# Sums of squares of keys and queries: from ones as a one-column moving tensor to ones as the stationary one

## What is computed

```python
proj = hn @ w_in
qkv = causal_conv_silu(proj[..., :A_CONV_CH], conv_w)        # 4 taps, then silu
q = l2_normalize(qkv[..., :A_KEY_W].reshape(bsz, s, 8, 128)) * 128 ** -0.5
k = l2_normalize(qkv[..., A_KEY_W:2 * A_KEY_W].reshape(bsz, s, 8, 128))
# l2_normalize(t) = t * rsqrt(sum(t * t over the 128 features of a head) + 1e-6)
o = gated_delta_rule(q, k, v, g, beta)       # in chunks; a unit lower triangular system is solved
```

## Time and profile before

| | us |
|---|---|
| median of three runs | 959.14 |
| span of the profiled execution | 957.3 |
| TensorE (PE) busy | 931.4 |
| VectorE (DVE) busy | 610.1 |
| ScalarE (ACT) busy | 497.3 |

### The profile page before, as it was taken

How to read it: one execution, slowest core, us unless ns; L and a number is a source line. 1 busy time by engine, 2 the same in 40 slices (tenths; PEclk the granted TensorE clock), 3 DMA queues, 4 the chain that set the end, 5 groups by cost and what they waited for, 6 DMA issues and landing times.

```text
span 957.3 us, 14052 instructions
## 1 busy us (share of the span) xinstructions
PE 931.4 (97%) x5304; PEld 795.4 (83%) x5304; DVE 610.1 (64%) x1037; ACT 497.3 (52%) x866; POOL 31.1 (3%) x43
## 2 busy tenths in 40 slices
PE   5999999999999999889999999999999999999998
PEld 5899989889989899667888888888877788888886
DVE  4787867767575687867645554546787664555443
ACT  4477541365465575656544444534675754444431
POOL 1001000000000001200000000001000000000000
PEclk9999989999999999999999999999999999999999
DMA  9353322255444555412566555654444256655550
GB/s 324 135 176 102 136 62 89 93 184 196 166 133 134 168 167 187 132 45 90 179 196 194 176 176 181 199 188 149 165 128 137 89 183 194 194 175 176 182 191 23
DMA packets 106294, 148.24 MB, mean 155 GB/s; under 512 B 12564, under 2 KB 59344, under 8 KB 106112
## 3 DMA queue, kind: packets, MB, share of 16 engines
q1 hardware_dynamic: 102014, 145.34, 47.1%
q0 software_dynamic: 704, 1.77, 0.5%
q10 hardware_dynamic: 3522, 0.39, 0.3%
HBM read 146.03 MB, written 1.45 MB: 154 GB/s over the span
## 4 chain that ended last, share of the span: by engine, by line
PE 88%; DVE 7%; ACT 3%; issue 1%; DMA 1%; SPq 0%; DVEq 0%; ACTq 0%
PE ps L1862 25%; PE ps L1864 24%; PE ps L1863 24%; PE ps L1957 4%; DVE wlo L1149 3%; ACT whi L636 1%; PE ps L2081 1%; PE ps L1997 1%; PE ps L2087 1%; PE ps L2235 1%; DMA C<-in_consts 1%; DVE G L1314 0%; PE ps L2443 0%; PE ps L2474 0%; PE ps L2039 0%
## 5 line engine op out<-in xcount | busy, mean ns | idle before, releaser
L1149 DVE TENSOR_TENSOR wlo<-raw,whi 128x1024 fp32r<-128x1024 f32 (+1 forms) x272 | 321.5, 1223 | 217.0 <-ACT whi L636 216.7
L636 ACT ACTIVATE whi<-raw 128x1024 fp32r<-128x1024 f32 (+1 forms) x272 | 271.3, 1045 | 274.3 <-PE ps L1864 273.6
L1862 PE MATMUL ps<-whi,xh 128*128 128x512 f32 (+1 forms) x544 | 217.4, 400 | 0.9 <-DVE wlo L1149 0.5
L1864 PE MATMUL ps<-whi,xl 128*128 128x512 f32 (+1 forms) x544 | 211.8, 389 | 0.0
L1863 PE MATMUL ps<-wlo,xh 128*128 128x512 f32 (+1 forms) x544 | 211.5, 389 | 0.0
L1862 PEld LDWEIGHTS ps<-whi,xh 128*128 128x128 f32 x544 | 102.2, 188 | 22.4 <-issue 2.6
L1864 PEld LDWEIGHTS ps<-whi,xl 128*128 128x128 f32 x544 | 102.1, 188 | 21.3
L1863 PEld LDWEIGHTS ps<-wlo,xh 128*128 128x128 f32 x544 | 102.4, 188 | 18.6
L1862 PE MATMUL ps<-xh,whi 128*128 128x256 f32 x384 | 112.9, 294 | 3.3 <-DVE xl L1215 3.0
L1863 PE MATMUL ps<-xl,whi 128*128 128x256 f32 x384 | 110.2, 287 | 0.0
L1864 PE MATMUL ps<-xh,wlo 128*128 128x256 f32 x384 | 110.1, 287 | 0.0
(11 more groups left out here) (391 smaller groups left out, 1191.3 us busy)
## 6 DMA issues: line engine op xcount, KB each, us to landing
raw<-in_l_w_gate SPq DMA_DIRECT2D x44, 512.0 KB, 3.9
raw<-in_l_w_up SPq DMA_DIRECT2D x44, 512.0 KB, 4.9
raw<-in_l_w_down SPq DMA_DIRECT2D x44, 512.0 KB, 4.6
raw<-in_l_w_in SPq DMA_DIRECT2D x36, 512.0 KB, 4.5
raw<-in_a_w_in SPq DMA_DIRECT2D x32, 512.0 KB, 4.7
raw<-in_w_kv SPq DMA_DIRECT2D x16, 512.0 KB, 4.7
raw<-in_b_w_in SPq DMA_DIRECT2D x16, 512.0 KB, 4.3
raw<-in_l_w_o SPq DMA_DIRECT2D x16, 512.0 KB, 4.4
```

Of the source, the lines that this page charges most:

```text
L636: nc.scalar.activation(whi[:, g % HIGH, a], raw[:, g % RAW, a], ACT.Copy).then_inc(hi_done, 1)
L1149: nc.vector.tensor_tensor(wlo[:, g % LOW, a], raw[:, g % RAW, a], whi[:, g % HIGH, a].bitcast(F32), ALU.subtract).then_inc(lo_done, 1)
L1862: mm(o_, a_h, b_h, start=start, stop=False, skip_group_check=True)
L1864: return mm(o_, a_l, b_h, start=False, stop=stop, skip_group_check=True)
```

## The change

The ones become the stationary operand, in quarters. `sum_rows(t)` multiplies `C[:, ONES:ONES + 32]` (128 rows, 32 columns of ones) with 512 columns of squares, four times, each time into another group of 32 partitions of bank 7. ScalarE copies the bank (128 by 512, `rows_summed`) to `G[:, 7]`, TensorE transposes the four tiles of the copy back into bank 7 (`sum_cols`), and VectorE reads one column in 32 of them (`summed`). For k the sums stay in slot 24 and the transposes are in slot 25. For q the sums move from behind slot 55 to slot 39, ScalarE's copy is in its slot 40 (behind the high part of a unit and the first tap of chunk 4), the transposes in slot 41, and the root of q with its scale in VectorE's slot 43. The old copy of line 814 and the waits for it go. The last KK quad now waits for VectorE's read alone, and the last KQ quad (slot 53) for its read of q.

```diff
-            def stats(t, b):
-                for h in range(HEADS):
-                    for tt in range(NT):
-                        k = 8 * tt + h
-                        last = mm(ps[:, b, k:k + 1], G[:, t, 256 * h + P * tt:256 * h + P * tt + P],
-                                  C[:, ONES:ONES + 1], start=True, stop=True)
-                    last.then_inc(S("qk_stat"), 1)
+            def sum_rows(t):
+                for j in range(4):
+                    last = mm(ps[32 * j:32 * j + 32, 7, :], C[:, ONES:ONES + 32], G[:, t, 512 * j:512 * j + 512],
+                              start=True, stop=True)
+                last.then_inc(S("row_sum"), 1)
+            def sum_cols(n):
+                pe.wait_ge(S("row_sb"), n + 1)
+                turn(S("col_sum"), 7, [row_sums(n)[:, P * i:P * i + P] for i in range(4)])
...
-                if s == KSTAT_AT:
+                if s == ROW_SUM_AT[0]:
                     pe.wait_ge(S("qk_sq"), 2)
                     pe.wait_ge(S("d_egb"), 4)
-                    stats(6, 7)
+                    sum_rows(6)
+                if s == ROW_SUM_AT[1]:
+                    pe.wait_ge(S("qk_sq"), 4)
+                    pe.wait_ge(S("a_mat"), 16)
+                    sum_rows(3)
+                for n in at_slot_of(COL_SUM_AT, s):
+                    sum_cols(n)
...
-            pe.wait_ge(S("qk_sq"), 4)
             pe.wait_ge(S("kk_d"), 8)
-            stats(3, 7)
```

On ScalarE (first two hunks) and VectorE (the rest):

```diff
+            def rows_summed(n):
+                act.wait_ge(S("row_sum"), n + 1)
+                nc.scalar.activation(row_sums(n), ps[:, 7, :], ACT.Copy).then_inc(S("row_sb"), 1)
...
-                if s == CONV_V + 1:
-                    act.wait_ge(S("qk_stat"), 16)
-                    nc.scalar.activation(rms["q"][2], ps[:, 7, 0:16], ACT.Copy).then_inc(S("q_stat"), 1)
...
+                if s == COL_SUM_AT[1] + 2:
+                    summed("q", 1)
+                    link(nc.vector.tensor_scalar(rq, rq, float(P) ** -0.5, None, ALU.mult))
...
-                if lv == 0:
-                    dve.wait_ge(S("q_stat"), 1)
-                    root("q", rms["q"][2], 1.0)
-                    link(nc.vector.tensor_scalar(rq, rq, float(P) ** -0.5, None, ALU.mult))
```

More of the change, by code:

```diff
@@ L253, in block_kernel @@
         QKV_SLOTS = 59
-        WAB_AT, AB_AT, GSUM_AT, KSTAT_AT = 5, 7, 10, 24
+        WAB_AT, AB_AT, GSUM_AT, ROW_SUM_AT, COL_SUM_AT = 5, 7, 10, (24, 39), (25, 41)
         SOLVE_AT, JOIN_AT, CONV_V = {45: (1, 5), 46: (5, HALF)}, 46, 55
@@ L260, in block_kernel @@
         by_head = lambda t: t.rearrange("p (h t d) -> p h t d", t=NT, d=P)
+        row_sums = lambda n: G[:, 7, 512 * n:512 * n + 512]
+        stat_ps = ps[:, 7, :].rearrange("p (e t j r) -> p t j e r", e=2, t=NT, j=4)[:, :, :, :, 0]
+        by_stat = lambda t: t.rearrange("p (t j e) -> p t j e", t=NT, j=4)
         FOX_CHUNKS = (0, 2, 4, 1, 3, 5)
@@ L746, in silu_z @@
                 act.wait_ge(unit_used, U_Z + 2 * c + 2)
-                act.wait_ge(S("qk_stat"), 16)
+                act.wait_ge(S("row_sum"), 2)
                 nc.scalar.activation(G[:, 3, :].rearrange("p (t n) -> p t n", t=NT)[:, :, 512 * c:512 * c + 512],
                                      ps[:, Z_BANK[c]:Z_BANK[c] + 2, :], ACT.Silu).then_inc(acc_read["A"], 1)
+            def rows_summed(n):
+                act.wait_ge(S("row_sum"), n + 1)
+                nc.scalar.activation(row_sums(n), ps[:, 7, :], ACT.Copy).then_inc(S("row_sb"), 1)
             def delta(s):
+                if s == ROW_SUM_AT[1] + 1:
+                    rows_summed(1)
                 if s == WAB_AT - 2:
@@ L818, in _ @@
                     hi_until(U_QKV + s // 4 + 2)
+                if s == ROW_SUM_AT[0]:
+                    rows_summed(0)
                 if s % 8 == 0 and 0 < s <= 48:
@@ L1349, in join, with summed @@
                 nc.vector.tensor_copy(blk(blk_y), blk(blk_x).rearrange("p i j -> p j i")).then_inc(S("solved"), 1)
+            def summed(name, n):
+                ms, y, t = rms[name]
+                dve.wait_ge(S("col_sum"), n + 1)
+                nc.vector.tensor_scalar(by_stat(ms), stat_ps, 1.0, EPS, ALU.mult, ALU.add).then_inc(S("stat_read"), 1)
+                dve.wait_ge(S("stat_read"), n + 1)
+                inverse_root(ms, y, t).then_inc(step(name, "root"), 1)
+                dve.wait_ge(*past(name, "root", 1))
             def delta(s):
@@ L1386, in delta @@
                             .then_inc(S("d_arg"), 1)
-                if s == KSTAT_AT + 1:
-                    dve.wait_ge(S("qk_stat"), 8)
-                    root("k", ps[:, 7, 0:16], 1.0)
+                if s == COL_SUM_AT[0]:
+                    summed("k", 0)
                     dve.wait_ge(S("gexp"), 2)
@@ L2036, in delta @@
                     if q_ == 3:
-                        pe.wait_ge(*past("k", "root", 1))
+                        pe.wait_ge(S("stat_read"), 1)
                     for n, a in enumerate(tiles(q_)):
@@ L2049, in delta @@
                     pe.wait_ge(S("kd"), 4 * min(q_, 1) + 4)
+                    if q_ == 3:
+                        pe.wait_ge(S("stat_read"), 2)
                     pe.wait_ge(S("a_mat"), 4 * q_ + 4)
@@ L2056, in delta @@
                     pe.wait_ge(S("kk_d"), 4 + q_ + 1)
-                    if q_ == 3:
-                        pe.wait_ge(S("q_stat"), 1)
                     turn(S("turned"), 4 + q_, [G[:, 2, a] for a in tiles(q_)])
```

## The result

The changed kernel takes 952.79 us, the median of five runs (951.48 to 954.44); the kernel before, run beside it, 959.14 us (958.71 to 959.42). The ratio is 0.9935, with a 95% interval of 0.9923 to 0.9947. The profiled execution after is the slowest of its five, 954.44 us; its span is 4.7 us shorter than that of before.

The account below looks back on a forecast made before the run. TensorE was taken as the bound from slot 24 to the sums of q. The dense stream's 1.7 us (3.5 - 1.8) shrank to 1.0 by t2's end, plus 0.65 for the root: 1.6 us, 959.14 to 957.5 us, range 955.1 to 959.6.

Parts of the forecast that it names:

- Four quarters run side by side: In each new sum on TensorE: four concurrent matmuls, 1.17 us with the change back; rival of quarters in turn, chance 0.13.
- The stage of k, 3.5 us: Slot 24 to the last KK quad: 3.5 us saved, the clock staying up behind the new sums.
- The sums of q add 1.8 us, the wait 0.2: Slots 39 to 43: 1.8 us added to the dense stream, including a new 0.2 us TensorE wait for ScalarE's copy.
- The root in slot 43: VectorE's root of q ahead of unit 12's low part, which starts at 103.4; 1.2 us of cover, so no cost.
- The last silu keeps its distance from the dense stream: ScalarE behind the dense stream: last silu ends 1.7 us earlier, at 128.7, just as the dense stream does.
- The clock behind the dense stream: TensorE idle behind the dense stream, so the clock falls as before, for 6.8 us from 128.6 to 135.4.
- a chance of 0.25 for another course: Rival behind the dense stream: clock stays up or returns sooner, 3.8 us gained in sum, 955.3 us; chance 0.25.
- The root off the path gives 1.0 us: From t2 of level 0 to t2 of level 1: 1.0 us saved without q's root on the path.
- The 0.35 us for the rest of the low clock: After t2 of level 0: low clock lasting up to 135.4 takes 0.35 us off the root's 1.0 us.
- the sum behind the dense stream: From the dense stream's end, 1.7 us earlier: t2 of level 0 ends 1.0 us earlier, plus 0.65, in sum 1.6 us.

Follow-up runs that it names:

- `full_width`: The changed kernel with the ones 128 columns wide instead of 32, so each of the four matmuls fills the whole array; 957.6 us, ratio 0.9989.
- `q_new`: The kernel before with only the sums of q in the new form and place, k keeping its thin matmuls; 956.94 us, ratio 0.998.
- `thin_moved`: The kernel before, both sums still thin one-column matmuls, but those of q moved to slot 39 and their root to slot 43; 959.78 us, ratio 1.0021.
- `before_pad128`: The kernel before with 128 repeated waits ahead of the first dense matmul, to have the code loaded at another moment; 958.48 us in one run.
- `k_new`: The kernel before with only the sums of k in the new form, q's thin matmuls staying behind slot 55; 951.52 us, then 952.35 us.
- `q_late`: `k_new` with the sums of q in the new form too, behind slot 55, copy and root on VectorE; 951.06 us, then 951.07 us.
- `after_fill`: The changed kernel with six unused matmuls of 512 columns behind slot 55, filling TensorE's gap ahead of t2; 953.34 us, ratio 0.9938.

## Why the prediction was wrong, point by point

- **Four quarters run side by side: right.** Forecast 1.17 us with the change back; measured 1.00 and 0.20, the KK quad behind taking 1.09 instead of 0.89. All sixteen matmuls of line 2012 have about 604 ns each, and the records of one group of four start 7 ns apart (62.200, 62.206, 62.213, 62.220). The Trainium skill, "TensorE: Matmul & The Clock Gate", "Measured speedup vs the span model", has 2.38 times for three; here four gave 3.44 / 1.00 = 3.4 times (`full_width`), better than its efficiency. That "TensorEngine Tiling (Array Packing)" of the Trainium skill, "Key Properties", has a drain at a change of mode agrees with the 0.20 us.
- **The stage of k, 3.5 us: right.** From 62.27 to 72.31 is 10.04 us, against 13.52. The clock stays at 1.00 there in every profile of the new form, and falls in each of the four with thin sums of k (before, `q_new`, `thin_moved`, `before_pad128`).
- **The sums of q add 1.8 us, the wait 0.2: right.** The transposes take 0.66 instead of 0.44. The dense stream, less the start's 1.0 us, ends 1.7 us earlier, as forecast. The root in slot 43 ends at 102.33, where the low part starts (forecast 103.4, less the 1.0), and TensorE waits for no low part there.
- **The last silu keeps its distance from the dense stream: wrong, 2.1 us.** I took the 3.47 us of issues in the earlier trace rows as a fixed price of that queue. They were held up by one transfer's landing, 4.0 us, of which a load of code took its share. The label "issue" hid this: the row says that the engine waited for nothing that the profile shows, and the DMA view would have shown the landing. `before_pad128` bears the cause out, and so do the packets of the transfer. Nothing in the change aims at it: with other instructions in the lists, the code is loaded at another moment. So this part of the gain is luck, and none of the new form's. It rests on one run with the load moved, on the packets, and on the landing after 1.8 to 2.1 us in every other profile. That all runs of the kernel before have the late landing isn't shown, since one of them was profiled; the two profiles of the changed kernel have the load at 126.68 and 126.70.
- **The clock behind the dense stream: half wrong.** In the profiled execution it fell for the forecast 6.8 us (forecast 128.6 to 135.4, measured 123.59 to 130.42), and cost 5.44 - 4.0 = 1.4 us between silu and p1. The length is right by luck: I counted the fall from when TensorE has nothing left behind its two quads, and it came 1.4 us before that, while they ran (122.00 to 124.97). Behind them TensorE was idle for 0.65 us, where I had 3.4. The sum had also taken it as equal before and after, with a chance of 0.25 for another course. It isn't: the table below shows it as different in kernels whose work there differs little, and from run to run.
- **The root off the path gives 1.0 us: right** (6.35 to 5.32). The 0.35 us for the rest of the low clock didn't come, since all was 4.5 us earlier and the clock was back before p1.
- **The step that failed in the whole** is thus the sum behind the dense stream, and in it the distance of the last silu, which was put at no change and measured 2.1 us. In the terms of the table above the forecast was 1.7 (dense) + 0 (silu) - 0.7 + 0.65 = 1.6; measured are 1.7 + 2.1 - 0.3 + 1.0 = 4.5, with 1.0 from the start, less 0.8 later, 4.7 of span. The other 1.65 us up to 6.35 lie between the median run and the profiled one, the slowest of five. In that set the time goes with the clock (951.48 and 951.77 us at 1.000, 954.03 and 954.44 at 0.996), in the second set it doesn't, so their cause stays open.

| kernel | mean clock of its runs | low, us a run | low stretches in its profiles, us |
|---|---|---|---|
| before, three sets beside the others | 0.993 to 0.994 | 11 to 13 | 3.4 (k), 6.8 (behind the dense stream) |
| `before_pad128`, one run | 0.998 | 4 | 3.4 (k) |
| `thin_moved` | 0.993 | 13 | 3.4, 3.4, 3.4 |
| `q_new` | 0.995 | 9 | 3.4 (k), 3.4 |
| changed, its own two sets | 0.997 to 0.998 | 4 to 6 | 6.8; 6.8 |
| `full_width` | 0.998 | 3 | none |
| `k_new`, two sets | 0.998 | 4 to 5 | none; none |
| `q_late`, two sets | 0.999, 1.000 | 2, 0 | none; none |

In `q_late` TensorE is idle for nearly half of 122 to 126 us (2.16 of 4.00 busy, in pieces of at most 1.1 us), and all five runs of its second set have a clock of 1.000. Filling the 1.5 us of the changed kernel in `after_fill` didn't keep the clock up. The Trainium skill, "TensorE: Matmul & The Clock Gate", "Why this matters for your kernels", has long idle gaps between bursts of matmuls lower the clock. No trace here can show it, since TensorE is never idle for more than 1.6 us at a time from 110 to 140 us; what they show is a fall without any idle time, behind the thin matmuls. In the dense stream these lowered it in all five places where a profile has them. Behind it they did so in before, and not in `before_pad128` and `k_new`. What lowers it behind the dense stream in the changed kernel and not in `q_late` stays open.

**Why the two parts don't add.** In the changed kernel TensorE's list carries 1.9 us for q in the dense stream, which is the path (1.00 of sums, 0.20 for the change back, 0.44 of transposes, 0.22 of waiting); behind it come 5.9 us up to the end of the last silu, with only four transposes and two quads for TensorE, in which the thin matmuls would have cost nothing (`k_new`). The move buys the root's 1.0 us and pays 1.9. `q_new` is faster than before all the same, by 1.8 us, since it has the early landing as well: 2.1 + 1.0 - 1.9 = 1.2 us, and 0.7 of clock between silu and p1 (5.10 to 4.43). And `k_new` has all of the gain: 3.5 for k, 2.0 for the landing (8.06 to 6.10) and 1.1 for the clock between silu and p1 (5.10 to 3.96) make 6.6 us, where 7.25 and in the second set 6.6 were measured.

## What to carry to other kernels

Sums over partitions by a stationary block of ones in four column quarters cost 1.0 us for 2048 columns of float32 (and 0.6 for turning them back and the change of form) where sixteen one-column matmuls cost 3.5 us and then 3.4 us at half the clock; put them where the tensor engine waits anyway, not in its dense stream. Before a wait named "issue" is carried over as a constant, look up the landing of the DMA that the queue waits for, and the packets of code beside it. Add one part's gain to another's only where both lie on the same path: here one part alone gave all.

## What the runs showed of the hardware that was not expected

- A load of 16 KB of code took 1.58 us, and a transfer of 128 KB that it fell into landed after 4.0 instead of 1.8 us; the last sixteenth of its packets started when the load was ending. The Trainium skill, "Runtime: NRT & Kernel Launch", "Instruction fetch mechanics", has code come in blocks of 16 KiB at a cost that is mostly hidden. The size agrees; here the cost fell on the transfer beside the load, and 2.1 us of it came onto the path.
- Four column quarters in float32 start 7 ns apart and take 1.00 us for two passes over 512 columns, 3.4 times less than in turn.
- Matmuls of one moving column lowered the granted clock to 0.5 for 3.4 us with TensorE busy throughout, in all four profiles that have them at slot 24; matmuls of 512 columns that took as long there (3.44 us, `full_width`) left it at 1.00.
- Between its first rise and the last 2 us of the program, the low clock has lengths of 3.4 and 6.8 us and no other in these profiles. It differs between runs of one kernel: the mean clock of before lies between 0.990 and 0.998.
